# Attention bias and band mask added by TensorE as a product of the identity, with one maximum over all 512 keys

## The reference

```
# L0, neighborhood attention: 256 queries of the latent stream against 256 latent keys and 256 context keys
s_win = q @ k_lat + bias          # bias from na_rpb; -1e30 outside the window of 16 columns
s_ctx = q @ k_ctx                 # nothing added
p = softmax(concat(s_win, s_ctx))
# and 256 context queries against the 256 context keys, nothing added

# L1, sliding window with a sink: 256 latent queries
s_win = where(|pos_q - pos_k| <= 128, q @ k_lat, -1e30)
s_ctx = q @ k_ctx
p = softmax(concat(s_win, s_ctx, sink of the head))
```

## Time and profile before

| | |
|---|---|
| median of 3 runs | 2973.15 us (2969.47 to 2976.09) |
| profiled execution | 2975.64 us, of which the span of the profile is 2974.0 us |
| TensorE matmul busy | 2711.8 us, 91% |
| VectorE busy | 1686.0 us, 57% |
| ScalarE busy | 1127.4 us, 38% |
| GpSimd busy | 339.4 us, 11% |
| mean granted TensorE clock | 0.946 |

### The profile page before, as it was taken

The page is one execution under the profiler, slowest core; times in us unless marked ns, Lnnn a source line. Parts: engine busy times, 40 slices in busy tenths (PEclk is TensorE's granted clock), DMA queues, the critical chain, the costliest instruction groups (busy, mean ns, idle before and its releaser), DMA issues.

```text
span 2974.0 us, 41244 instructions
## 1 busy us (share of the span) xinstructions
PE 2711.8 (91%) x16084; PEld 2311.8 (78%) x16084; DVE 1686.0 (57%) x2700; ACT 1127.4 (38%) x1523; POOL 339.4 (11%) x411
## 2 busy tenths in 40 slices
PE   6999989998999999999989999888569999965999
PEld 3888867866888868888866899888459999952999
DVE  4744646785653746747458555655445655643555
ACT  3222242374222223212246534544334554433453
POOL 3000041223100022000210201000002000000100
PEclk8999999999999999999999999998679999966999
DMA  6533515402442523545320455444015454400444
GB/s 247 168 136 118 185 57 198 156 30 71 156 163 99 180 96 126 185 135 181 116 85 1 153 180 186 160 146 151 1 44 183 170 177 177 174 20 0 172 169 149
DMA packets 64495, 394.19 MB, mean 133 GB/s; under 512 B 7424, under 2 KB 8928, under 8 KB 29280
## 3 DMA queue, kind: packets, MB, share of 16 engines
q1 hardware_dynamic: 41648, 310.09, 29.6%
q0 software_dynamic: 21008, 76.03, 7.7%
q10 hardware_dynamic: 1696, 6.08, 0.5%
HBM read 391.13 MB, written 1.05 MB: 132 GB/s over the span
## 4 chain that ended last, share of the span: by engine, by line
PE 81%; DVE 10%; ACT 5%; issue 2%; DMA 1%; POOL 1%; ACTq 0%; DVEq 0%; POOLq 0%
PE banks L404 22%; PE banks L405 22%; PE banks L406 22%; DVE wlo L369 2%; ACT whi L361 2%; PE banks L1055 2%; PE banks L1043 2%; PE banks L1033 1%; PE banks L429 1%; PE banks L431 1%; PE banks L430 1%; DMA scale_start<-in_w_mod_scale 1%; PE banks L419 1%; PE banks L420 1%; PE banks L421 1%
## 5 line engine op out<-in xcount | busy, mean ns | idle before, releaser
L369 DVE TENSOR_TENSOR wlo<-raw,whi 128x2048 fp32r<-128x2048 f32 (+1 forms) x272 | 667.3, 2453 | 461.2 <-ACT whi L361 461.2
L361 ACT CAST whi<-raw 128x2048 fp32r<-128x2048 f32 (+1 forms) x272 | 548.4, 2016 | 260.6 <-PE banks L406 213.2
L404 PE MATMUL banks<-uhi,whi 128*128 128x512 f32 (+1 forms) x1648 | 602.3, 365 | 3.1 <-DVE wlo L369 3.1
L405 PE MATMUL banks<-ulo,whi 128*128 128x512 f32 (+1 forms) x1648 | 601.1, 365 | 0.0
L406 PE MATMUL banks<-uhi,wlo 128*128 128x512 f32 (+1 forms) x1648 | 601.0, 365 | 0.0
L404 PE MATMUL banks<-u2hi,whi 128*128 128x256 f32 x1312 | 371.5, 283 | 6.1 <-DVE wlo L369 3.6
L405 PE MATMUL banks<-u2lo,whi 128*128 128x256 f32 x1312 | 370.1, 282 | 0.0
L406 PE MATMUL banks<-u2hi,wlo 128*128 128x256 f32 x1312 | 370.1, 282 | 0.0
L404 PEld LDWEIGHTS banks<-uhi,whi 128*128 128x128 f32 x1648 | 310.1, 188 | 58.9 <-DVE wlo L369 3.6
L406 PEld LDWEIGHTS banks<-uhi,wlo 128*128 128x128 f32 x1648 | 310.3, 188 | 54.8
L405 PEld LDWEIGHTS banks<-ulo,whi 128*128 128x128 f32 x1648 | 310.3, 188 | 54.7
(11 more groups left out here) (369 smaller groups left out, 4113.3 us busy)
## 6 DMA issues: line engine op xcount, KB each, us to landing
raw<-in_ffn_in SPq DMA_DIRECT2D x132, 1024.0 KB, 4.8
raw<-in_ffn_out SPq DMA_DIRECT2D x48, 1408.0 KB, 6.3
mod_slot<-in_w_mod POOLq DMA_DIRECT2D x128, 512.0 KB, 3.6
raw<-in_w_merge SPq DMA_DIRECT2D x32, 1024.0 KB, 4.8
raw<-in_w_in SPq DMA_DIRECT2D x26, 1024.0 KB, 4.8
raw<-in_na_qkv SPq DMA_DIRECT2D x12, 1024.0 KB, 4.7
raw<-in_w_out SPq DMA_DIRECT2D x8, 1024.0 KB, 4.8
raw<-in_wa_qkv SPq DMA_DIRECT2D x6, 1024.0 KB, 4.8
```

What stands on the lines that cost most here:

```text
L361: act.copy(whi[u % 2][:, 0:unit_size[u]], raw[u % 2][:, 0:unit_size[u]]).then_inc(hi_done, 1)
L369: dve.tensor_tensor(wlo[u % 2][:, 0:n], raw[u % 2][:, 0:n], whi[u % 2][:, 0:n].bitcast(F32), ALU.subtract).then_inc(lo_done, 1)
L404: pe.matmul(out, w_hi, x_hi[:, k, 0:T], start=(n == 0), stop=False)
L405: pe.matmul(out, w_hi, x_lo[:, k, 0:T], start=False, stop=False)
```

## The change

For steps with a bias or a mask, TensorE computes after the scores of both sides another product into the same bank, without clearing it: the 128x128 identity times the 128x256 bias. The wait for the bias moves from VectorE to TensorE. VectorE then finds the maximum of all 512 keys with one reduce; in L1 a second instruction over one column takes the sink in and negates. The load of the next bias waits for TensorE's step instead of VectorE's. The causal mask of the third attention is added by VectorE as before.

```diff
 def scores(n):
...
             for side, t in enumerate(steps[n]["tiles"]):
-                pe.matmul(banks[:, score_bank(n, side), 0:steps[n]["n"]], t["q"], t["k"], start=True, stop=True)\
-                    .then_inc(*PE_.up((tag, "scores", n)))
+                mm = pe.matmul(banks[:, score_bank(n, side), 0:steps[n]["n"]], t["q"], t["k"], start=True, stop=True)
+                if t["bias"] is None:
+                    mm.then_inc(*PE_.up((tag, "scores", n)))
+            for side, t in enumerate(steps[n]["tiles"]):
+                if t["bias"] is not None:
+                    pe.wait_ge(*t["bias ready"])
+                    pe.matmul(banks[:, score_bank(n, side), 0:S], ident, t["bias"],
+                              start=False, stop=True, skip_group_check=True).then_inc(*PE_.up((tag, "scores", n)))
...
 def attention_max_dve(dve, tag, n, side, t):
-        if t["added"] is None:
+        if t["scale"] != 1.0:
+            part = sc[:, 0:t["causal"].shape[-1]]
+            dve.scalar_tensor_tensor(part, part, t["scale"], t["causal"], ALU.mult, ALU.add).then_inc(*DVE_.up())
+            dve.wait_ge(*DVE_.here())
+        if t["sink"] is None:
             dve.tensor_reduce(nmax, sc, AX.X, ALU.max, negate=True).then_inc(*DVE_.up((tag, "max", n, side)))
             return
-        if t["added ready"] is not None:
-            dve.wait_ge(*t["added ready"])
-        w = t["added"].shape[-1]
-        part = sc[:, 0:w]
-        floor = NEG if t["sink"] is None else t["sink"]
-        if t["scale"] == 1.0:
-            dve.tensor_tensor_reduce(part, part, t["added"], 1.0, floor, ALU.add, ALU.max, nmax)\
-                .then_inc(*DVE_.up((tag, "added", n, side)))
-        else:
...
-        if w_all > w:
-            dve.tensor_reduce(other, sc[:, w:], AX.X, ALU.max).then_inc(*DVE_.up())
-            dve.wait_ge(*DVE_.here())
-            dve.tensor_scalar(nmax, nmax, other, -1.0, ALU.max, ALU.mult)\
-                .then_inc(*DVE_.up((tag, "max", n, side)))
+        dve.tensor_reduce(other, sc, AX.X, ALU.max).then_inc(*DVE_.up())
+        dve.wait_ge(*DVE_.here())
+        dve.tensor_scalar(nmax, other, t["sink"], -1.0, ALU.max, ALU.mult).then_inc(*DVE_.up((tag, "max", n, side)))
...
 def na_steps():
-                    tiles[-1]["added ready"] = POOL_.at("bias", hd) if t == 0 else None
+                    tiles[-1]["bias ready"] = POOL_.at("bias", hd)
...
 def wa_steps():
-                    tiles[-1]["added ready"] = None
+                    tiles[-1]["bias ready"] = (window_loaded, 16)
...
 def bias_pool(pool):
-                pool.wait_ge(*DVE_.at("L0", "added", 4 * (ck - 1) + 1, 1))
+                pool.wait_ge(*PE_.at("L0", "scores", 4 * (ck - 1) + 1))
```

More of the change, by code:

```diff
@@ L1107, in attention_max_dve @@
         nmax, other = small[:, i:i + 1], small[:, 120 + i:121 + i]
-        if t["added"] is None:
+        if t["scale"] != 1.0:
[3 more added lines that the diff above has]
+        if t["sink"] is None:
             dve.tensor_reduce(nmax, sc, AX.X, ALU.max, negate=True).then_inc(*DVE_.up((tag, "max", n, side)))
             return
-        if t["added ready"] is not None:
-            dve.wait_ge(*t["added ready"])
-        w = t["added"].shape[-1]
-        part = sc[:, 0:w]
-        floor = NEG if t["sink"] is None else t["sink"]
-        if t["scale"] == 1.0:
-            dve.tensor_tensor_reduce(part, part, t["added"], 1.0, floor, ALU.add, ALU.max, nmax)\
-                .then_inc(*DVE_.up((tag, "added", n, side)))
-        else:
-            dve.scalar_tensor_tensor(part, part, t["scale"], t["added"], ALU.mult, ALU.add)\
-                .then_inc(*DVE_.up((tag, "added", n, side)))
-            dve.wait_ge(*DVE_.here())
-            dve.tensor_reduce(nmax, sc, AX.X, ALU.max, negate=True).then_inc(*DVE_.up((tag, "max", n, side)))
-        if w_all > w:
-            dve.tensor_reduce(other, sc[:, w:], AX.X, ALU.max).then_inc(*DVE_.up())
-            dve.wait_ge(*DVE_.here())
-            dve.tensor_scalar(nmax, nmax, other, -1.0, ALU.max, ALU.mult)\
-                .then_inc(*DVE_.up((tag, "max", n, side)))
+        dve.tensor_reduce(other, sc, AX.X, ALU.max).then_inc(*DVE_.up())
+        dve.wait_ge(*DVE_.here())
+        dve.tensor_scalar(nmax, other, t["sink"], -1.0, ALU.max, ALU.mult).then_inc(*DVE_.up((tag, "max", n, side)))
     def attention_dve(dve, tag, steps, y_hi, y_lo):
@@ L1173, in na_steps @@
                         q=qT[p0:p0 + HD, ck, t * P:(t + 1) * P], k=kT[p0:p0 + HD, ck, k0:T2], n=T2 - k0,
-                        added=na_bias[ck % 2][:, side, t * S:(t + 1) * S] if t < 2 else None, scale=1.0, sink=None,
+                        bias=na_bias[ck % 2][:, side, t * S:(t + 1) * S] if t < 2 else None, scale=1.0, sink=None,
                         v=[vv[:, kt, hd * HD:(hd + 1) * HD] for kt in range(k0 // P, 4)], at=(p0, t * P)))
-                    tiles[-1]["added ready"] = POOL_.at("bias", hd) if t == 0 else None
+                    tiles[-1]["bias ready"] = POOL_.at("bias", hd)
                 steps.append(step(tiles, group=ck, chunk=ck, first=(t == 0), last=(t == 3), width=T2, most=T2))
@@ L1190, in wa_steps @@
                         q=qT[p0:p0 + HD, ck, t * P:(t + 1) * P], k=kT[p0:p0 + HD, ck // 4, 0:T2], n=T2,
-                        added=c("wa_mask")[:, t * S:(t + 1) * S], scale=1.0, sink=sinks[:, hd:hd + 1],
+                        bias=c("wa_mask")[:, t * S:(t + 1) * S], scale=1.0, sink=sinks[:, hd:hd + 1],
                         v=[vv[:, kt, kv * HD:(kv + 1) * HD] for kt in range(4)], at=(p0, t * P)))
-                    tiles[-1]["added ready"] = None
+                    tiles[-1]["bias ready"] = (window_loaded, 16)
                 steps.append(step(tiles, group=ck, chunk=ck, first=(t == 0), last=(t == 1), width=S, most=T2))
@@ L1206, in mla_steps @@
                         q=qk[0:QK, hd, t * P:(t + 1) * P], k=qk[0:QK, 4 + hd, 0:n], n=n,
-                        added=c("causal")[:, t * S:t * S + n], scale=QK ** -0.5, sink=None,
+                        bias=None, causal=c("causal")[:, t * S:t * S + n], scale=QK ** -0.5, sink=None,
                         v=[mla_v[:, kt, hd * HD:(hd + 1) * HD] for kt in range(t + 1)], at=(HD * side, t * P)))
-                    tiles[-1]["added ready"] = None
                 steps.append(step(tiles, group=pair, chunk=6 + pair, first=(t == 0), last=(t == 1), width=S, most=S))
```

## The result

The changed kernel takes 3001.59 us (median of 4 runs, 2999.93 to 3009.75) against 2973.56 us for the kernel before (4 runs, 2969.47 to 2976.09). The ratio is 1.0101 with a 95% interval of 1.0079 to 1.0123: 1.0% slower. The forecast was 2996.8 with a range to 3008. Between the medians lie 28.0 us, where 23.6 were forecast. The profiled execution took 2999.93 us, the fastest of the four, with a span of 2998.3, so between the two profiled executions lie 24.3 us.

A forecast was written before the change was run, and what follows sets the result against it. The prediction took TensorE to bound the kernel, with one VectorE wait per L0 group. Its terms, 8.1 + 1.5 + 9.5 + 4.5, summed to +23.6 us on the median of 2973.15, giving 2996.8 us, range 2987 to 3008.

The forecast's parts named there:

- What bounds the kernel: Whole kernel: TensorE sets the pace, with one VectorE wait of 0.93 us per L0 group and 0.10 per L1 round.
- A pair costs 0.90: TensorE, L0 and L1: the two heads' identity products of a step add 0.90 us, with 1.05 as near upper value.
- Rivals 2 and 3: Identity products: each pays its own start, 1.2 to 1.4 us a pair, 3008 (13%); or cheap, 0.51 a pair, 2984 (4%).
- VectorE's relief 0.65 a pair: VectorE, L0: the two maxima of a step fall from 1.86 to 1.21 us with single reduces over 512.
- A group of L0 +1.15: Steady L0: two pairs add 1.80 us, the wait falls by 0.65; seven groups give +8.1 us.
- The load's new release costed at nothing: Next bias load, waiting for TensorE's scores instead of VectorE's add: no cost, with some 15 us of cover.
- Fill of L0 1.5: Start of L0: TensorE waits for GpSimd's first masks; +1.0 us at full clock, up to +2.8 at half, 1.5 taken.
- A round of L1 +0.80: Steady L1: a round goes from 3.695 to 4.49 us; 12 rounds give +9.5 us.
- Fill of L1 4.5: Start of L1: bias pairs of steps 0 to 3, partly at half clock, add 3.1 to 5.8 us, 4.5 taken.
- rival 1: Starts of L1 and L0: products keep TensorE's clock from halving, 3.5 and 1 us come back, 2992 (20%).
- The sum: Whole kernel: steady L0 8.1, L0 fill 1.5, steady L1 9.5 and L1 fill 4.5 make +23.6 us.

The follow-up runs named there:

- the late load: The changed kernel, with GpSimd issuing the next bias load only after VectorE has normalised step t=1 of the group before: 2999.01 us, ratio 1.0076.
- filler: Products of constants added on TensorE among and after the rotary products before L1: on the kernel before 2975.93 us, ratio 1.0003; on the changed kernel 3004.60 us, ratio 1.0098.

## Why the prediction came out as it did

- *What bounds the kernel:* right. With VectorE's extra work put back (both engines add) L1's rounds don't change at all (the stage by 0.6, in its fill) and L0 by 0.66 us a group; with the identity products doubled the whole follows, by 28 us.
- *A pair costs 0.90:* right, 0.91 net in the changed kernel, 0.86 for one more in a stream. Rivals 2 and 3, a start for each product and the half price, fall with the doubled products.
- *VectorE's relief 0.65 a pair:* right (1.86 to 1.21).
- *A group of L0 +1.15:* nearly. Free of contention it is 13.17 against 11.885, +1.29. The wait fell by 0.53 and not by 0.65, because the scores of t=1 reach VectorE 1.02 us later (2.22 after their start, it was 1.20), while TensorE itself loses only 0.91.
- *The load's new release costed at nothing:* this is the step that failed. I checked that the masked bias comes in time, and it does; I didn't ask what the masking runs beside. It came to lie on the normalisation of t=1, which is on the way to TensorE's transposes: 0.69 us a group on average (13.86 against 13.17), 4.2 us in the six groups and up to 7 in another execution. The trace before could have warned me: a scaling of 256 columns takes 0.89 us beside a mask there (shown with the late load), and the normalisation of t=1 ends at 630.41, just as the next mask has begun at 630.20.
- *Fill of L0 1.5:* too small, 3.2 in these two traces. The scores of step 1 and their pair ran at half clock, so that the upper end of my bound (2.8) was the likelier: to the first transposes it lost 3.0. And 0.7 of the 3.2 is contention again, which the term doesn't have. Without it and at like clock (the late load) the fill loses 1.4 to 1.8.
- *A round of L1 +0.80:* right, +0.81 in 11 rounds (8.9 us).
- *Fill of L1 4.5:* too large. To the scores of step 4 it took 16.18 us instead of 14.60, and with the end of the stage it lost 1.9. Before, the clock was at half for some 10 us in two pieces around a full one; in the changed kernel it was at half once, for 6.8 us (1579.9 to 1586.7). The other traces agree: one piece of 6.8 us in all six with the changed L1 and no filler, 10.2 us in all five without identity products in L1 and without filler. So rival 1 came true in part, for L1 only. With filler, and the first scores at full clock in both, the products of the fill cost 0.6 us: they fit in waits.
- *The sum:* 8.1 + 1.5 + 9.5 + 4.5 became 7.7 for six groups without contention, 4.2 for the contention in them, 1.3 for the last group, 3.2 for the fill of L0, 8.9 for L1's rounds and 1.9 for its fill and end, 27.2. An error of +7 in L0 and one of -3 in L1 stand against each other. All these are from one execution of each kernel. In the others the changed L0 took up to 5 us more and the old one up to 1.7, so how near the total came to the forecast is chance as well.

## What to carry to other kernels

Price a move from one engine to another by what each is waiting for: here an instruction on VectorE was worth something in one of the four steps of a group, and TensorE had 0.1 us a round to spare for 0.9. When a transfer or an operation of a side engine gets a new release, ask not only whether it still comes in time but what it will run beside. If a product has to carry a bias, do it only in the step whose maximum stands on the critical chain, and in fp32r if the bias can bear the rounding (0.28 us net a pair against 0.91).

## What the runs showed of the hardware

GpSimd's elementwise work and VectorE's slow each other. VectorE's scaling of 128x512 within SBUF took 0.49 us alone and up to 1.52 us beside GpSimd's masking (1.60 with the change in L0 alone), and GpSimd's mask of two tiles 2.67 to 2.97 us instead of the 2.48 to 2.50 with the late load. In the same groups VectorE's reads of PSUM kept their time (with the late load the two maxima at 590.21 took 1.29 beside the mask at 589.12, the 1.29 they take without one). The Trainium skill, page "GPSIMD Engine Reference", section "Specifications", has GpSimd's SBUF interface shared with VectorE, with contention when VectorE's instruction runs in a two-port performance mode or has two SBUF inputs; the longer times of both engines agree with a shared interface. The scaling has one SBUF input, and no trace shows whether it runs in a two-port mode; the maxima, which read PSUM, were not slowed.

The granted clock isn't the same in every execution of the same code: in the fill of L0 as before it was at half for 3.4 us in one trace and for 6.8 in two others, and the fill took 12.4 us against 13.7 and 14.1.

Filler in TensorE's idle time kept the granted clock full where it had been half: the first two pairs of scores in L1 took 1.99 us instead of 3.54, at the price of nothing in the stage ahead of them (12.3 us from the first rotary product to the first scores, 12.2 without it).
